# A second modulation panel multiplied in two halves around the first projection chunk

## The chip, the cores and the metric

The kernel runs on one core of one Trainium2 chip. The metric is the device time of one execution in microseconds (us). Before the change the median of three runs is 671.01 us (669.97 to 671.13).

## The reference, cut to what matters

One layer of a hybrid diffusion backbone works on 512 latent and 128 context tokens, each a row of 1024 numbers. Everything is float32. The part that the change touches is the beginning:

```
mod = SiLU(cond) @ w_mod + b_mod      # shift1, scale1, gate1, shift2, scale2, gate2; cond: c (latent), c_ctx (context)
h   = RMSNorm_pre1(x) * (1 + scale1) + shift1
z   = h @ w_in                        # columns [q | k | v | B | C | u], 512 each
```

Attention (four heads with differential softmax), a short gated convolution, the projection w_o, a second norm with shift2 and scale2 and a mixture of 16 experts follow. Lambda, a scalar of the attention, comes from two dot products of 64 numbers and an exponential.

## The kernel before, in words

The engines run lists of instructions written out by hand, one for each engine; each engine issues its list in order, and semaphores tie them together. There is no planner: the order of the calls in the code is the order of the work.

The first stage makes h, transposed and split into two float32r parts (high and low), and multiplies it by the first 512 columns of w_in. The 1024 numbers of a row are cut into eight **chunks** k of 128. Chunk k of h needs its columns of shift1 and scale1; these come in four **panels** n, panel n holding the columns of chunks 2n and 2n+1. The steps and their names are:

- `mod_early(n)` (TensorE, L1726): panel n of w_mod times the two conditioning vectors, eight steps over k, in four row groups of one PSUM bank. Its weights come in four quarters, each by two transfers of SyncE's queue (L467), into eight slots; between the panels SyncE fetches the quarters of w_in (L494).
- `mod_rows_out(n)` (VectorE, L1214): adds the bias and copies the result out of PSUM.
- `mod_cols(n)` (TensorE, L1734): transposes it, so that shift and scale lie along partitions.
- `mod_columns(n)` (VectorE, L1220 to L1226): sums the row groups and makes A1 and B1; its last instruction raises `a1_ready`.
- `h_transposes(k)` (TensorE, L1770) and `ctx_transposes(f)` (L1763): transposes of the normed x into PSUM, latent tokens a chunk at a time, context tokens four chunks at a time.
- `h_chunk(k)` (ScalarE, L802 and L806): scales and shifts the latent rows of chunk k, then rounds the chunk to the high part. It waits for `a1_ready` and for the transposes of its chunk. `h_ctx(k)` (VectorE, L1236) scales the context rows.
- `h_lo(k)` (VectorE, L1241): the low part of chunk k; raises `hT_ctx`.
- `split_hi` (ScalarE, L787) and `split_lo` (VectorE, L1207): high and low part of a quarter of w_in.
- `z_first(k)` (TensorE, L1779): chunk k for the first three blocks of 128 tokens, three matmuls of 512 columns each, accumulated over the chunks in three PSUM banks. It waits for `hT_ctx`.

TensorE's order is: panel 0, transposes of the context and of chunks 0 and 1, columns 0, the two dot products for lambda (L1796, L1797), panel 1, chunk 0, columns 1, transposes 2 and 3, chunk 1, panel 2, chunk 2, columns 2, transposes of the context and of 4 and 5, chunk 3, panel 3, chunk 4, columns 3, transposes 6 and 7, chunks 5, 6 and 7. Then `z_rows(3)` (L1846) and the rest of the projections follow. VectorE's order for n from 1 is: rows of panel n out, low part of chunk 2n-1, low part of the quarter, columns, context rows of 2n, low part of 2n, context rows of 2n+1.

Of the kernel before, what the change touches and what calls it, by code (L numbers as in the profile page):

```python
# [29 lines left out]
P = 128  # L30
D = 1024
KC = D // P
# [4 lines left out]
H, DV, DQ = 4, 128, 64  # L37
# [9 lines left out]
MOD_EARLY = 4  # L47
# [16 lines left out]
def build(nc, a):  # L64
# [16 lines left out]
    with ctx:  # L81
        def sb(name, shape, dt=F32):
            return ctx.enter_context(nc.sbuf_tensor(name, shape, dt))
# [20 lines left out]
        ones = sb("ones", [P, P])  # L104
# [7 lines left out]
        ps = ctx.enter_context(nc.psum_tensor("ps", [P, 8, N], F32))  # L112
# [14 lines left out]
        def col(i, n=1):  # L127
            return small[:, i:i + n]
# [7 lines left out]
        lamp = col(99)  # L136
        nlam = col(100)
        epsc = col(101)
        lamw = col(102, 4)
# [81 lines left out]
        def early_slot(j):  # L221
            return qkv[:, (j % 8) * D:(j % 8 + 1) * D]
# [952 lines left out]
        def _(dve):  # L1175
            n_chain = [0]

            def link(ins):
                n_chain[0] += 1
                ins.then_inc(S["dve_chain"], 1)  # L1180
                dve.wait_ge(S["dve_chain"], n_chain[0])
# [10 lines left out]
            link(nc.vector.tensor_copy(small[:, 16:39], ps[:, 6, 0:23]))  # L1192
            link(ts(subg, subg, 1.0 - LAM_INIT, None, ALU.mult))
            tt(lamp, lamq[:, 0:1], lamq[:, 1:2], ALU.mult).then_inc(S["lam_prod"], 1)

            dve.wait_ge(S["rms1"], 1)
            link(nc.vector.reciprocal(rstd, rt))
# [3 lines left out]
            def split_lo(item):  # L1201
                kind, c, r = item
                n = place[kind, c]
                m = 6 * P if kind == "conv" else QUARTER
                slot, rslot = (4 * n + r) % SPLIT, at_ring[item] % RAW
                dve.wait_ge(S["hi"], 4 * n + r + 1)
                tt(spl[:, slot, 1, 0:m], raw[:, rslot, 0:m], spl[:, slot, 0, 0:m].bitcast(F32), ALU.subtract).then_inc(S["lo"], 1)  # L1207

            def mod_rows_out(n):
                dve.wait_ge(S["mod_q"], 4 * (n + 1))  # L1210
                if n >= 2:
                    dve.wait_ge(S["col_mm"], n - 1)
                both = lambda ap, m: ap.rearrange("p (s n) -> p s n", s=2)[:, :, m:m + CHUNK]
                tt(both(rows_early[n % 2], 0), both(ps[:, 4 + n % 2, :], 0), both(bias_early, n * CHUNK), ALU.add).then_inc(S["mod_ev"], 1)  # L1214

            def mod_columns(n):
                dve.wait_ge(S["col_mm"], n + 1)
                ks = slice(2 * n, 2 * n + 2)
                parts = ps[:, 4 + n % 2, :].rearrange("p (j g m) -> p j m g", j=4, g=4)[:, :, 0:2, :]
                link(nc.vector.reduce_sum(cols_early.rearrange("p (j c) -> p j c", c=2), parts, axis=AX))  # L1220
                sh = cols_early[:, 0:4].rearrange("p (k c) -> p c k", c=2)
                sc = cols_early[:, 4:8].rearrange("p (k c) -> p c k", c=2)
                nc.vector.tensor_copy(B1[:, :, ks], sh)
                stt(A1[:, 0, ks], sc[:, 0, :], 1.0, gpre1[:, ks], ALU.add, ALU.mult)
                link(stt(A1[:, 1, ks], sc[:, 1, :], 1.0, gpre1[:, ks], ALU.add, ALU.mult))
                ts(col(183), epsc, 1.0, None, ALU.mult).then_inc(S["a1_ready"], 1)  # L1226

            def hf_rows(k):
                return work[:, TOK * (k % 2):TOK * (k % 2 + 1)]

            def h_ctx(k):
                dve.wait_ge(S["h_trc"], k // 4 + 1)
                if k >= 2:
                    dve.wait_ge(S["hT_ctx"], k - 1)
                o = (k % 4) * P
                ts(hf_rows(k)[:, L_LAT:TOK], ps[:, 2, o:o + P], A1[:, 1, k:k + 1], B1[:, 1, k:k + 1],  # L1236
                   ALU.mult, ALU.add).then_inc(S["hf_ctx"], 1)

            def h_lo(k):
                dve.wait_ge(S["hT_lat"], k + 1)  # L1240
                tt(hS[:, 1, k, :], hf_rows(k), hS[:, 0, k, :].bitcast(F32), ALU.subtract).then_inc(S["hT_ctx"], 1)  # L1241
            dve.wait_ge(S["bmod_in"], 16)
            mod_rows_out(0)
            split_lo(("in", 0, 0))
            mod_columns(0)
            h_ctx(0)
            h_ctx(1)
            h_lo(0)
            dve.wait_ge(S["lam_mm"], 1)
            nc.vector.tensor_copy(lamw[:, 0:1], ps[:, 6, 0:1]).then_inc(S["lam_cp"], 1)  # L1250
            nc.vector.tensor_copy(lamw[:, 1:2], ps[:, 3, 0:1]).then_inc(S["lam_cp"], 1)
            for n in range(1, MOD_EARLY):
                mod_rows_out(n)
                h_lo(2 * n - 1)
                split_lo(("in", 0, n))
                mod_columns(n)
                h_ctx(2 * n)
                h_lo(2 * n)
                h_ctx(2 * n + 1)
            h_lo(KC - 1)  # L1260
            split_lo(SPLITS[2][0])

            def rope_rows(g):
# [446 lines left out]
        def _(pe):  # L1710
            mm = nc.tensor.matmul
# [3 lines left out]
                    pe.wait_ge(S["lo"], 4 * n + k // 2 + 1)  # L1715
            PASSES = ((0, 0), (0, 1), (1, 0))

            def mod_early(n):
                if n >= 2:
                    pe.wait_ge(S["a1_ready"], n - 1)  # L1720
                for k in range(KC):
                    j = 4 * n + k // 2
                    if k % 2 == 0:
                        pe.wait_ge(early[j % 8], 32 * (j // 8 + 1))
                    g = 32 * (k % 4)
                    ins = mm(ps[g:g + 32, 4 + n % 2, :], condz[:, k, :], early_slot(j)[:, (k % 2) * N:(k % 2 + 1) * N],  # L1726
                             start=(k < 4), stop=(k >= 4))
                    if k % 2:
                        ins.then_inc(S["mod_q"], 1)

            def mod_cols(n):
                pe.wait_ge(S["mod_ev"], n + 1)
                for j in range(4):
                    ins = nc.tensor.transpose(ps[:, 4 + n % 2, j * P:(j + 1) * P], rows_early[n % 2][:, j * P:(j + 1) * P], ident[:, :])  # L1734
                ins.then_inc(S["col_mm"], 1)
# [20 lines left out]
            def ctx_transposes(f):  # L1756
                if f == 0:
                    pe.wait_ge(S["xn_ready"], TB)
                else:
                    pe.wait_ge(S["hf_ctx"], 4)  # L1760
                for j in range(4):
                    k = 4 * f + j
                    ins = nc.tensor.transpose(ps[:, 2, j * P:(j + 1) * P], x[:, CTX, k * P:(k + 1) * P], ident[:, :])  # L1763
                ins.then_inc(S["h_trc"], 1)

            def h_transposes(k):
                if k >= 2:
                    pe.wait_ge(S["hf_lat"], k - 1)
                for b in range(4):
                    ins = nc.tensor.transpose(ps[:, k % 2, b * P:(b + 1) * P], x[:, b, k * P:(k + 1) * P], ident[:, :])  # L1770
                ins.then_inc(S["h_tr"], 1)

            def z_first(k):
                n = place["in", 0]
                pe.wait_ge(S["hT_ctx"], k + 1)
                part_ready(n, k)
                for g, bank in enumerate((3, 6, 7)):
                    for s, m in PASSES:
                        ins = mm(ps[:, bank, :], hS[:, s, k, g * P:(g + 1) * P], weight(n, k, m),  # L1779
                                 start=(k == 0 and s + m == 0), stop=(k == KC - 1 and s == 1))  # L1780
                    if k == KC - 1:
                        ins.then_inc(S["z_mm"], 1)
# [4 lines left out]
            pe.wait_ge(S["stage_in"], 16 * 7)  # L1787
            nc.tensor.transpose(ps[:, 6, 0:23], vrow, ident[0:23, 0:23]).then_inc(S["rows_tr"], 1)
            pe.wait_ge(S["cols_ready"], 2)
            mod_early(0)  # L1790
            ctx_transposes(0)
            h_transposes(0)
            h_transposes(1)
            mod_cols(0)
            pe.wait_ge(S["lam_prod"], 1)
            mm(ps[:, 6, 0:1], ones[0:DQ, :], lamp[0:DQ, :], start=True, stop=True)  # L1796
            mm(ps[:, 3, 0:1], ones[DQ:P, :], lamp[DQ:P, :], start=True, stop=True).then_inc(S["lam_mm"], 1)  # L1797
            mod_early(1)
            pe.wait_ge(S["lam_cp"], 2)
            z_first(0)  # L1800
            mod_cols(1)
            h_transposes(2)
            h_transposes(3)
            z_first(1)
            mod_early(2)
            z_first(2)
            mod_cols(2)
            ctx_transposes(1)
            h_transposes(4)
            h_transposes(5)  # L1810
            z_first(3)
            mod_early(3)
            z_first(4)
            mod_cols(3)
            h_transposes(6)
            h_transposes(7)
            z_first(5)
            z_first(6)
            z_first(7)

# [452 lines left out]
```

## Time and profile before

| | |
|---|---|
| median of three runs | 671.01 us |
| profiled execution | 670.32 us |
| its span | 668.3 us |
| TensorE busy | 638.8 us (96% of the span) |
| VectorE busy | 511.7 us (77%) |
| ScalarE busy | 415.9 us (62%) |
| moved by DMA | 188.16 MB, mean 282 GB/s |

The span is the time from the first to the last instruction that the profile shows; the execution's own time lies some 2 us above it. PE is TensorE's matmuls, PEld its weight loads, DVE is VectorE, ACT is ScalarE, SP is SyncE's queue. A float32 matmul appears as several records, so the panel's eight steps are 16 records. A chain entry or a timeline line merges neighbouring instructions of a line of the code.

### The profile page before, as it was taken

The numbers are of one execution on the slowest core, as the hardware profiler recorded it, in microseconds if no ns is written. First come the engines' busy times: TensorE is split into PE (matmuls) and PEld (weight loads), VectorE is DVE, ScalarE is ACT, GpSimd is POOL, SyncE is SP. The second block draws the span as 40 slices with busy tenths as digits, with TensorE's granted clock in tenths as the row PEclk, the third lists the DMA queues.
The fourth block names the chain that finished last, engine by engine and source line by source line (L and its number), as shares of the span: only waits on it lengthen the run. The fifth ranks groups of instructions, "written<-read, shape, count | busy, mean of one in ns | idle before, by whom it ended". The sixth has DMA issues, their size and how long they took to land.

```text
span 668.3 us, 11051 instructions
## 1 busy us (share of the span) xinstructions
PE 638.8 (96%) x3570; PEld 524.4 (78%) x3570; DVE 511.7 (77%) x755; ACT 415.9 (62%) x640; POOL 106.1 (16%) x172
## 2 busy tenths in 40 slices
PE   3999999999999999999998999999999999999993
PEld 0577767889999998888786788888888888888871
DVE  2666576757676767775778989898989899999976
ACT  5552122344747486763447588888888888888863
POOL 2041000065000000000014500000000000370341
PEclk9999999999999999999999999999999999999997
DMA  9975768549211134495499799999999999999776
GB/s 332 386 248 186 262 242 254 156 147 339 60 38 57 63 97 156 138 332 191 147 323 346 237 415 419 420 420 420 420 420 419 418 410 415 416 404 375 302 273 157
DMA packets 77147, 188.16 MB, mean 282 GB/s; under 512 B 7823, under 2 KB 29380, under 8 KB 77108
## 3 DMA queue, kind: packets, MB, share of 16 engines
q1 hardware_dynamic: 65408, 153.11, 61.7%
q0 software_dynamic: 7392, 22.47, 9.9%
q10 hardware_dynamic: 4310, 12.10, 4.5%
q8 instruction: 22, 0.36, 0.2%
q14 instruction: 15, 0.12, 0.1%
HBM read 166.12 MB, written 21.53 MB: 281 GB/s over the span
## 4 chain that ended last, share of the span: by engine, by line
PE 81%; DVE 6%; DMA 5%; ACT 2%; SPq 2%; issue 2%; POOL 1%; ACTq 0%; DVEq 0%; POOLq 0%
PE ps L2135 23%; PE ps L2155 12%; PE ps L1846 10%; PE ps L1870 7%; PE ps L1902 6%; PE ps L1874 5%; PE ps L1923 3%; PE ps L1946 2%; PE ps L1779 2%; PE ps L2111 2%; SPq L467 2%; PE ps L1937 2%; DMA catT_mem<-token_rows,token_lists 1%; PE ps L1744 1%; DMA catT_mem<-expert_rows,early_slots 1%
## 5 line engine op out<-in xcount | busy, mean ns | idle before, releaser
L2135 PE MATMUL ps<-split_ring,split_rows 128*128 128x512 f32 x714 | 167.0, 392 | 0.1
L1492 DVE TENSOR_TENSOR split_ring<-qkv_mem,split_ring 128x1024 fp32r<-128x1024 f32 x123 | 142.9, 1221 | 23.2 <-ACT split_ring L975 23.2
L2135 PEld LDWEIGHTS ps<-split_ring,split_rows 128*128 128x128 f32 x714 | 132.7, 188 | 28.2 <-DVE split_ring L1492 0.5
L975 ACT CAST split_ring<-qkv_mem 128x1024 fp32r<-128x1024 f32 x123 | 120.1, 1053 | 9.3 <-ACT catT_mem L1081 9.3
L1870 PE MATMUL ps<-split_rows,split_ring 128*128 128x384 f32 x288 | 87.1, 349 | 0.2 <-ACT work L910 0.2
L2155 PE MATMUL ps<-split_ring,split_rows 128*128 128x512 f32 x360 | 86.4, 395 | 0.0
L2155 PEld LDWEIGHTS ps<-split_ring,split_rows 128*128 128x128 f32 x360 | 66.6, 188 | 13.7
L1874 PE MATMUL ps<-split_rows,split_ring 128*128 128x256 f32 x288 | 77.0, 280 | 0.0
L1492 DVE TENSOR_TENSOR split_ring<-raw_ring,split_ring 128x1024 fp32r<-128x1024 f32 x64 | 74.2, 1218 | 0.0
L1846 PE MATMUL ps<-split_ring,split_rows 128*128 128x512 f32 x288 | 68.0, 393 | 0.0
L975 ACT CAST split_ring<-raw_ring 128x1024 fp32r<-128x1024 f32 x64 | 62.4, 1047 | 1.2 <-DMA raw_ring<-in_w_exp_up 1.2
L1846 PEld LDWEIGHTS ps<-split_ring,split_rows 128*128 128x128 f32 x288 | 53.4, 188 | 10.8
L787 ACT CAST split_ring<-raw_ring 128x1024 fp32r<-128x1024 f32 (+1 forms) x36 | 34.2, 958 | 40.7 <-DMA raw_ring<-in_w_in 40.7
L1902 PE MATMUL ps<-split_ring,split_rows 128*128 128x512 f32 x240 | 58.4, 396 | 0.7 <-DVE split_ring L1207 0.7
L1207 DVE TENSOR_TENSOR split_ring<-raw_ring,split_ring 128x1024 fp32r<-128x1024 f32 (+1 forms) x36 | 39.4, 1102 | 23.1 <-ACT split_ring L787 22.9
L1870 PEld LDWEIGHTS ps<-split_rows,split_ring 128*128 128x128 f32 x288 | 53.5, 189 | 1.4 <-issue 1.2
L1874 PEld LDWEIGHTS ps<-split_rows,split_ring 128*128 128x128 f32 x288 | 53.4, 188 | 0.0
L1902 PEld LDWEIGHTS ps<-split_ring,split_rows 128*128 128x128 f32 x240 | 44.0, 188 | 10.4 <-DVE split_ring L1207 1.0
L1348 DVE TENSOR_REDUCE small<-ps 128x1 f32<-128x640 f32 (+1 forms) x40 | 26.8, 712 | 12.9 <-PE ps L1923 12.7
L631 POOL DMA_DIRECT2D x_rows<-in_b_mod x10 | 5.1, 512 | 181.7 <-DMA out_lat<-x_rows 181.7
L679 POOL TENSOR_TENSOR rows_now<-token_lists 128x1 uint32<-128x1 uint32 x13 | 4.8, 368 | 182.2 <-PE ps L2111 182.2
L878 ACT COPY x_rows<-ps 128x640 f32<-128x640 f32 (+1 forms) x20 | 12.2, 612 | 32.0 <-PE ps L1937 31.9
(363 smaller groups left out, 924.3 us busy)
## 6 DMA issues: line engine op xcount, KB each, us to landing
qkv_mem<-in_w_exp_gate SPq DMA_DIRECT2D x64, 512.0 KB, 8.4
qkv_mem<-in_w_exp_up SPq DMA_DIRECT2D x60, 512.0 KB, 7.0
raw_ring<-in_w_exp_down SPq DMA_DIRECT2D x60, 512.0 KB, 8.3
raw_ring<-in_w_mod SPq DMA_DIRECT2D x26, 512.0 KB, 4.2
qkv_mem<-in_w_mod SPq DMA_DIRECT2D x32, 256.0 KB, 7.0
expert_rows<-catT_mem ACTq DMA_DIRECT2D x14, 512.0 KB, 6.6
expert_rows<-work POOLq DMA_DIRECT2D x26, 256.0 KB, 5.8
raw_ring<-in_w_in SPq DMA_DIRECT2D x12, 512.0 KB, 6.9
```

The source lines that it names most:

```text
L787: nc.scalar.copy(spl[:, (4 * n + r) % SPLIT, 0, 0:m], raw[:, q % RAW, 0:m]).then_inc(S["hi"], 1)
L975: nc.scalar.copy(moe_split(tile, j, r, 0), moe_raw(tile, j, r)).then_inc(S["hi"], 1)
L1207: tt(spl[:, slot, 1, 0:m], raw[:, rslot, 0:m], spl[:, slot, 0, 0:m].bitcast(F32), ALU.subtract).then_inc(S["lo"], 1)
L1348: nc.vector.reduce_max(nm[:, u % 2, c:c + 1], psf[:, SC[c]:SC[c] + nk], axis=AX, negate=True).then_inc(S["neg_max"], 1)
L1492: tt(moe_split(tile, j, r, 1), moe_raw(tile, j, r), moe_split(tile, j, r, 0).bitcast(F32), ALU.subtract).then_inc(S["lo"], 1)
L1846: ins = mm(ps[:, g % 2, :], hS[:, s, k, b * P:(b + 1) * P], weight(n, k, m), start=(k == 0 and s + m == 0), stop=(k == KC - 1 and s == 1))
L1870: return mm(ps[:, CONV_BANK, 0:LOW], conv_weight(n, k, s, part), hS[:, m, k, 0:LOW], start=(k == 0 and s + m == 0), stop=(k == KC - 1 and ...
L1874: return mm(ps[:, CONV_BANK + 1, 0:HIGH], conv_weight(n, k, s, part), hS[:, m, k, LOW:TOK], start=(k == 0 and s + m == 0), stop=(k == KC - ...
L1902: ins = mm(ps[:, banks + j, :], cS[:, s, b, kk, :], weight(place["o", j], kk, m), start=(kk == 0 and s + m == 0), stop=(kk == KC - 1 and s ...
L1923: ins = mm(psf[:, SC[c] + o:SC[c] + o + m], q[rows, :], key[rows, :], start=(s + w == 0), stop=(s == 1))
L2135: ins = mm(ps[:, j, :], rows[:, s, k * P:(k + 1) * P], moe_split(tile, j, k // 2, m)[:, (k % 2) * N:(k % 2 + 1) * N], start=(k == 0 and s ...
L2155: ins = mm(ps[:, 5 + half, :], aS[:, s, k, :], spl[:, moe_split_slot(turn, j, k), m, half * N:(half + 1) * N], start=(k == 0 and s + m == ...
```

## The change

Four things are reordered; no arithmetic is added or taken away.

1. The two dot products for lambda and VectorE's two copies of them go ahead of panel 0.
2. Columns 0 go ahead of the transposes of chunk 1. Panel 1 is cut into steps 0 to 3, which stay ahead of chunk 0, and steps 4 to 7, which go behind it.
3. Columns 1, 2 and 3 go into the middle of a chunk (1, 3 and 4), between its first block of tokens and the other two. Panel 2 goes behind chunk 2, panel 3 ahead of chunk 4 and behind chunk 3, the transposes of chunks 6 and 7 behind chunk 5.
4. VectorE's order becomes, for every n: rows out, columns, context rows of 2n, low part of the quarter, low part of 2n, context rows of 2n+1, low part of 2n+1.

```diff
 # VectorE
+            dve.wait_ge(S["lam_mm"], 1)
+            nc.vector.tensor_copy(lamw[:, 0:1], ps[:, 6, 0:1]).then_inc(S["lam_cp"], 1)
+            nc.vector.tensor_copy(lamw[:, 1:2], ps[:, 3, 0:1]).then_inc(S["lam_cp"], 1)
             dve.wait_ge(S["rms1"], 1)
...
-            mod_rows_out(0)
-            split_lo(("in", 0, 0))
-            mod_columns(0)
-            h_ctx(0)
-            h_ctx(1)
-            h_lo(0)
...
-            for n in range(1, MOD_EARLY):
+            for n in range(MOD_EARLY):
                 mod_rows_out(n)
-                h_lo(2 * n - 1)
-                split_lo(("in", 0, n))
                 mod_columns(n)
                 h_ctx(2 * n)
+                split_lo(("in", 0, n))
                 h_lo(2 * n)
                 h_ctx(2 * n + 1)
-            h_lo(KC - 1)
+                h_lo(2 * n + 1)
 # TensorE
-            def mod_early(n):
+            def mod_early(n, ks=range(KC)):
-            def z_first(k):
+            def z_first(k, gs=range(3)):
...
             pe.wait_ge(S["cols_ready"], 2)
+            pe.wait_ge(S["lam_prod"], 1)
+            mm(ps[:, 6, 0:1], ones[0:DQ, :], lamp[0:DQ, :], start=True, stop=True)
+            mm(ps[:, 3, 0:1], ones[DQ:P, :], lamp[DQ:P, :], start=True, stop=True).then_inc(S["lam_mm"], 1)
             mod_early(0)
             ctx_transposes(0)
             h_transposes(0)
+            mod_cols(0)
             h_transposes(1)
-            mod_cols(0)
...
-            mod_early(1)
+            mod_early(1, range(4))
             pe.wait_ge(S["lam_cp"], 2)
             z_first(0)
+            mod_early(1, range(4, KC))
+            h_transposes(2)
+            z_first(1, (0,))
             mod_cols(1)
-            h_transposes(2)
+            z_first(1, (1, 2))
             h_transposes(3)
-            z_first(1)
+            z_first(2)
             mod_early(2)
-            z_first(2)
+            z_first(3, (0,))
             mod_cols(2)
+            z_first(3, (1, 2))
             ctx_transposes(1)
             h_transposes(4)
             h_transposes(5)
-            z_first(3)
             mod_early(3)
-            z_first(4)
+            z_first(4, (0,))
             mod_cols(3)
+            z_first(4, (1, 2))
+            z_first(5)
             h_transposes(6)
             h_transposes(7)
-            z_first(5)
             z_first(6)
             z_first(7)
```

## Rows read from the trace of the kernel before

**Rows 1.** The page: busy times of the engines, and the chain by engine.
```profile
PE 638.8 (96%) x3570; PEld 524.4 (78%) x3570; DVE 511.7 (77%) x755; ACT 415.9 (62%) x640; POOL 106.1 (16%) x172
...
PE 81%; DVE 6%; DMA 5%; ACT 2%; SPq 2%; issue 2%; POOL 1%; ACTq 0%; DVEq 0%; POOLq 0%
```
**Rows 2.** Waits of PE after 49 us: total, times, longest.
```profile
PE ps L2111 <- DMA catT_mem<-token_rows,token_lists: 2.4, 1, 2.4
```
**Rows 3.** Windows: length, busy us of each engine, granted clock, DMA share, GB/s.
```profile
12.00:24.00 12.00, 11.05 (x53) 3.55 (x54) 7.74 (x19) 5.41 (x8) 0.00 (x0) 1.00 1.08 389
24.00:38.00 14.00, 14.00 (x88) 10.07 (x91) 9.30 (x22) 7.29 (x10) 0.00 (x0) 1.00 1.08 392
...
80.00:120.00 40.00, 40.00 (x199) 29.62 (x199) 28.56 (x41) 10.49 (x16) 1.98 (x4) 1.00 0.77 250
```
**Rows 4.** Timeline of PE, first stage: start, us, instructions, idle before and releaser.
```profile
12.16 4.96 PE L1726 MATMUL ps<-qkv_mem,cond_columns 128*32 128x512 f32 x16 [2.59 <-DMA qkv_mem<-in_w_mod]
...
17.71 1.04 PE L1770 MATMUL ps<-ident,x_rows 128*128 128x128 f32 x8
18.58 0.60 PE L1734 MATMUL ps<-ident,catT_mem 128*128 128x128 f32 x4
19.11 0.27 PE L1796 MATMUL ps<-small,ones 64*128 64x1 f32 x1
...
19.43 1.70 PE L1726 MATMUL ps<-qkv_mem,cond_columns 128*32 128x512 f32 x8
...
20.07 0.14 PEld L1726 LDWEIGHTS ps<-qkv_mem,cond_columns 128*32 128x32 f32 x4 [0.50 <-DMA qkv_mem<-in_w_mod]
...
22.82 1.05 PE L1726 MATMUL ps<-qkv_mem,cond_columns 128*32 128x512 f32 x4 [0.30 <-DMA qkv_mem<-in_w_mod]
...
45.32 4.45 PE L1779 MATMUL ps<-split_ring,split_rows 128*128 128x512 f32 x18 [0.28 <-DVE split_rows L1241]
```
**Rows 5.** Chain of waits, 31 to 50 us: start, us, what.
```profile
31.39 2.27 PE ps L1779 x9
...
34.54 0.87 PE ps L1770 x8
...
37.48 1.85 PE ps L1726 x16
...
41.64 0.45 PE ps L1734 x4
...
42.87 0.79 ACT work L802
...
44.43 0.84 DVE split_rows L1241
```
**Rows 6.** Timeline of ACT and DVE around chunk 4.
```profile
35.06 0.78 ACT L802 ACTIVATE work<-ps,small 128x512 f32<-128x512 f32 x1 [3.16 <-PE ps L1770]
36.63 0.82 DVE L1241 TENSOR_TENSOR split_rows<-work,split_rows 128x640 fp32r<-128x640 f32 x1 [1.43 <-ACT split_rows L806]
37.37 0.40 DVE L1236 TENSOR_SCALAR work<-ps,small 128x128 f32<-128x128 f32 x1
37.87 0.72 ACT L806 CAST split_rows<-work 128x640 fp32r<-128x640 f32 x1 [0.59 <-DVE work L1236]
39.43 0.69 DVE L1214 TENSOR_TENSOR catT_mem<-ps,catT_mem 128x512 f32<-128x512 f32 x1 [1.65 <-PE ps L1726]
```
**Rows 7.** Timeline of DVE, 13 to 20 us.
```profile
13.53 0.19 DVE L1197 RECIPROCAL small<-small 128x5 f32<-128x5 f32 x1 [3.36 <-ACT small L792]
17.23 0.69 DVE L1214 TENSOR_TENSOR catT_mem<-ps,catT_mem 128x512 f32<-128x512 f32 x1
18.42 1.23 DVE L1207 TENSOR_TENSOR split_ring<-raw_ring,split_ring 128x1024 fp32r<-128x1024 f32 x1 [0.49 <-ACT split_ring L787]
```
**Rows 8.** Timeline of SyncE's queue: issues of the fourth panel.
```profile
24.38 5.84 SPq L467 DMA_DIRECT2D qkv_mem<-in_w_mod  x8
```
**Rows 9.** Transfers: issues, KB each, median us to landing.
```profile
qkv_mem<-in_w_mod SPq DMA_DIRECT2D x32, 256.0 KB, 7.0
```

More of the change, by code:

```diff
@@ L1242, in _ @@
             dve.wait_ge(S["bmod_in"], 16)
-            mod_rows_out(0)
-            split_lo(("in", 0, 0))
-            mod_columns(0)
-            h_ctx(0)
-            h_ctx(1)
-            h_lo(0)
-            dve.wait_ge(S["lam_mm"], 1)
-            nc.vector.tensor_copy(lamw[:, 0:1], ps[:, 6, 0:1]).then_inc(S["lam_cp"], 1)
-            nc.vector.tensor_copy(lamw[:, 1:2], ps[:, 3, 0:1]).then_inc(S["lam_cp"], 1)
-            for n in range(1, MOD_EARLY):
+            for n in range(MOD_EARLY):
                 mod_rows_out(n)
-                h_lo(2 * n - 1)
-                split_lo(("in", 0, n))
                 mod_columns(n)
                 h_ctx(2 * n)
+                split_lo(("in", 0, n))
                 h_lo(2 * n)
                 h_ctx(2 * n + 1)
-            h_lo(KC - 1)
+                h_lo(2 * n + 1)
             split_lo(SPLITS[2][0])
@@ L1716, in _ @@
             PASSES = ((0, 0), (0, 1), (1, 0))
-            def mod_early(n):
+            def mod_early(n, ks=range(KC)):
                 if n >= 2:
                     pe.wait_ge(S["a1_ready"], n - 1)
-                for k in range(KC):
+                for k in ks:
                     j = 4 * n + k // 2
@@ L1776, in z_first @@
                 part_ready(n, k)
-                for g, bank in enumerate((3, 6, 7)):
+                for g in gs:
+                    bank = (3, 6, 7)[g]
                     for s, m in PASSES:
@@ L1792, in _ @@
             h_transposes(0)
+            mod_cols(0)
             h_transposes(1)
-            mod_cols(0)
-            pe.wait_ge(S["lam_prod"], 1)
-            mm(ps[:, 6, 0:1], ones[0:DQ, :], lamp[0:DQ, :], start=True, stop=True)
-            mm(ps[:, 3, 0:1], ones[DQ:P, :], lamp[DQ:P, :], start=True, stop=True).then_inc(S["lam_mm"], 1)
-            mod_early(1)
+            mod_early(1, range(4))
             pe.wait_ge(S["lam_cp"], 2)
             z_first(0)
+            mod_early(1, range(4, KC))
+            h_transposes(2)
+            z_first(1, (0,))
             mod_cols(1)
-            h_transposes(2)
+            z_first(1, (1, 2))
             h_transposes(3)
-            z_first(1)
+            z_first(2)
             mod_early(2)
-            z_first(2)
+            z_first(3, (0,))
             mod_cols(2)
+            z_first(3, (1, 2))
             ctx_transposes(1)
```

## The prediction

> **What bounds the kernel now.** I read the page first: TensorE (PE) is busy for 96% of the span, and PE makes up 81% of the chain that ended last [rows 1]. So time is lost or won where PE stands still. The list of PE's waits after 49 us comes second: the longest is 2.4 us [rows 2]. Windows of the projections behind the first stage show PE busy throughout, 40.00 of 40 us from 80 to 120 [rows 3], so a shift of the first stage should run through to the end. Third, the timeline of PE in the first stage. Panel 0 of the modulation weights ends at 17.12 us. Panel 1 then runs in pieces: eight records from 19.43, its second quarter's weight load at 20.07 and its last four records at 22.82, with "DMA qkv_mem" named as what ended the gaps [rows 4]. Here PE waits for weights. The DMA share of this stretch is 1.08, and the stream stays full until 38 us [rows 3]. The reader is to see a wait of about 3 us ahead of the first projection chunk (23.87 us, that is 22.82 and 1.05 more), that PE is then busy for all of the window from 24 to 38 [rows 3], and a gap of 0.28 us before chunk 6 at 45.32 [rows 4]. Fourth, the chain of waits around that small gap. It goes from the last columns (mod_cols 3, ends 42.09) through DVE's reduction and A1 to ACT's scaled copy (42.87), and through ACT's rounding cast and DVE's low part (44.43) to chunk 6 [rows 5]. That is **3.23 us from the end of the columns to the first matmul that can use them**. The same path from the end of the transposes of a chunk, when its columns are long there, can be read at chunk 4: the pair of transposes begins at 34.54 and takes 0.87, so chunk 4's end at 34.97; ACT starts at 35.06, the low part ends at 37.45 [rows 6]. With 0.05 us to PE (the low part before chunk 6 ends at 45.27, chunk 6 starts at 45.32 [rows 4, 5]) that is **2.53 us from the end of the transposes**. Both latencies are now covered by work that PE has in between. The question for every moved line is whether that cover stays.
>
> **The change, part by part.** All times are those of the profiled execution (span 668.30, its own time 670.32). The work of PE is the same; what is moved decides.
>
> *Lambda.* The records of L1796 and L1797 leave PE's path between 19.11 and 19.43 [rows 4], which is 0.3 us. They go to before 12.16, where PE stood idle 2.59 us; the two small DVE copies go into DVE's idle 3.36 us before 13.53 [rows 7]. Cost nothing, and if that cover were gone 0.3 us.
>
> *Columns of panel 0 ahead of the second transposes.* A group of four transposes costs 0.44 (mod_cols 3: 41.64 to 42.09 [rows 5]). After the context transposes and one group from 17.71, mod_cols(0) runs at 18.14 instead of 18.58 [rows 4]; its operand is ready at 17.92, as the evacuation begins at 17.23 and takes 0.69 [rows 7]. It ends at 18.58, and 3.23 later, 21.81, the first chunk may start. On DVE the quarter's low part (1.23 us [rows 7]) now stands behind the context rows and fits exactly into the time in which ACT works.
>
> *Panel 1 in halves.* The first half needs the second quarter, which landed at 20.07 [rows 4], and is done by 21. The first chunk goes at 21.81 instead of 23.87: **2.06 us won**. A chunk takes 2.27 (from 31.39 [rows 5]), so it ends at 24.08. The second half follows. The trace has no half of a panel with its data there. Bounds: 0.92 (not less, as the matmuls are the same), half of the 1.85 of panel 3 (37.48 to 39.34 [rows 5]), and 1.05, a single quarter alone [rows 4]. I take 0.92, since all four row groups are filled as in a whole panel. It ends at 25.0 against 23.87: the panel is 1.1 late, but one chunk ahead.
>
> *Columns inside chunks, to chunk 2.* Transposes to 25.4, a third of chunk 1 to 26.1, mod_cols(1) to 26.55 (before: 26.57). Chunk 2 can start 3.23 later, at 29.78. Ahead of it PE has two thirds of chunk 1 (1.33: six of nine matmuls in the 2.07 that a chunk takes behind transposes: 35.41, where the pair from 34.54 ends, to 37.48 [rows 5]) and one group of transposes: done at 28.3. **PE waits 1.5.** Before, panel 2 filled this time; now it stands behind chunk 2. Chunk 2 ends at 32.05, panel 2 at 33.9. Before, the same work was done at 33.66 (31.39 and 2.27 [rows 5]): the lead is gone, +0.2.
>
> *Chunk 3 and panel 3.* A third of chunk 3 (0.76) to 34.66. The evacuation of panel 2 takes 0.09 to start, 0.69 and 0.05 to PE, so mod_cols(2) runs from 34.73 to 35.17. The rest of chunk 3 to 36.5, context transposes, transposes of chunk 4 to **37.37** and of 5 to 37.8, panel 3 to 39.65 (before 39.34). Its weights are no limit: the fourth panel was issued by 30.2 and a quarter takes 7.0 us to land [rows 8, 9], so the last is there near 37.2, before 37.8. Chunk 4 may start 2.53 after its transposes, at 39.9: a wait of 0.25. Its first third ends at 40.66.
>
> *mod_cols(3) and DVE's order.* mod_cols(3) needs DVE's evacuation of panel 3. In the new order of DVE that stands **behind the low part of chunk 5**, which was behind it before (evacuation at 39.43 [rows 6]). From 37.37 the path is: low part of 4 (ends +2.48), context rows of 5 (begin +2.40), cast of 5 (+2.90 to +3.62), low part of 5 (from +3.65), evacuation (from +4.38, ends +5.07), PE at +5.11. These offsets are those of rows 6 against 34.97, with the low part and the evacuation changing places. So mod_cols(3) starts at 42.48, and **PE waits 1.8**; behind it in PE's order are all the chunks that could run. It ends at 42.92. Two thirds of chunk 4 to 44.25, chunk 5 to 46.52.
>
> *Transposes of chunks 6 and 7 behind chunk 5.* They stood ahead of it, and chunk 5 covered the 2.53 us. Now chunk 6's end at 46.96, chunk 7's at 47.4, and chunk 6 can start at 49.49: **PE waits 2.1**. For chunk 7 ACT and DVE have the 2.2 us of chunk 6; before it ran on without a gap, 18 matmuls in 4.45 [rows 4], so the stage ends at 53.94 against 49.77.
>
> The sum is +4.2 us. Queues: SP's quarters of panel 3 wait for panel 1's matmuls, at the latest for 25.0, and the later half of panel 3 was issued after 27 [rows 8]; POOL's loads behind the last A1 start 0.9 later, and what uses them, behind chunk 7, moves by 4.2. The bounds on the parts: each of the three paths (3.23, 5.11, 2.53) could be 0.1 shorter (two of its wakes of 0.05 gone) or 0.4 longer (half of the low part of a quarter, 1.23 [rows 7], in DVE's way); with the half panel, 0.13, that is +3.9 to +5.5.
>
> *The clock.* In 12 to 24 us the granted clock is 1.00, the 2.4 GHz level, though PE waited for DMA several times [rows 3]. The Trainium skill ("TensorE: Matmul & The Clock Gate", section "HAM oscillation — how this bites in real kernels") warns that matmul bursts with waits between them can fall back to the half clock; this trace does not show it here, and it is a rival below.
>
> **The rivals.** *B, not slower:* the waits before chunk 2, mod_cols(3) and chunk 6 don't appear, because what bounds those chunks is only the columns, which now come earlier relative to the matmuls that use them. For it: the chain of before leads from A1 to ACT for chunk 6 (ACT starts at 42.87, 0.78 behind the columns' end [rows 5]). Against it: ACT also needs the transposes, and those of 6 are issued behind chunk 5. The new waits sum to 5.7, so without them 4.2 - 5.7 = -1.5, or 669.5 on the median. It decides when these waits stay under 1.5 in all.
>
> *C, given back later:* a later wait of PE that doesn't move with PE swallows a part. The longest is the 2.4 us for gathered token rows [rows 2]; this leaves +1.8, 672.8. Against it: that gather starts from rows that PE's own results produce, so it moves along.
>
> *D, the clock falls in the waits:* after the waits of 1.8 and 2.1 us the last 18 matmuls run at 1.2 GHz. The trace has no such row; at half the clock their 4.45 is doubled (an estimate from that row), +8.6, 679.7.
>
> *E, the stream sets the stage:* if the weights' landing, not PE, fixed the stage's end, nothing changes, 671.0. Against it: after 23.87 PE has no gap until 38 us [rows 3], and the one before 45.32 ended on DVE [rows 4].
>
> **How the numbers follow.** The profiled execution took 670.32, 0.7 below the median of 671.01. On the median, 671.01 + 4.2 = 675.2. Chances: forecast 0.75 (own range 674.6 to 676.5), B 0.09, C 0.08, D 0.03, E 0.05. The range from 672.6 to 676.7 takes in the forecast and C and leaves out B, D and E. About 0.2%, 1.3 us, can be told from no change: faster 0.09 (B), the same 0.05 (E), slower 0.86 (forecast, C, D).
>
> **What would show it.** In the changed profile the first L1779 starts near 21.8 (right: the halves work). A gap of PE of 1.5 before the third chunk; a gap of 1.8 before the last L1734, with DVE's L1214 running right behind an L1241 and not ahead of it; a gap of 2.1 before the last 18 L1779, ended by L1241; the first L1846 near 54 instead of 49.6, and the same spacing from there to the end. I am wrong if the last 18 L1779 follow the transposes without a gap, if L1846 starts before 50, or if the later list of waits has shrunk by what the first stage lost.

## The result, and the profile after

The changed kernel takes 676.48 us in the median of seven runs (673.24 to 678.48), the kernel before in the same comparison 669.97 (668.79 to 671.13). The ratio is 1.0091, with an interval from 1.0074 to 1.0108: it is **slower by 6.1 us**, between 5.0 and 7.2. Forecast were 4.2 us and 675.2; the direction and the three waits were right, the size was too small.

The page of the changed kernel, busy times and chain by engine, and below it PE's longest wait behind the first stage, answer to [rows 1, 2]:

```profile
PE 640.6 (95%) x3570; PEld 525.7 (78%) x3570; DVE 512.1 (76%) x755; ACT 416.2 (62%) x640; POOL 106.3 (16%) x172
...
PE 83%; DVE 7%; ACT 4%; issue 3%; DMA 1%; ACTq 1%; DVEq 0%; POOLq 0%
```
```profile
PE ps L2109 <- DMA catT_mem<-token_rows,token_lists: 2.4, 1, 2.4
```

PE has the same number of instructions, 1.8 us more of busy time, and a smaller share of a longer span. The wait for token rows is 2.4 us as before: nothing was given back there. The timeline of PE in the first stage (start, us, instructions, idle before and its releaser) answers to [rows 4]; L1719 is mod_early, L1727 mod_cols, L1763 the transposes, L1773 z_first, L1844 the first z_rows:

```profile
22.13 2.31 PE L1773 MATMUL ps<-split_ring,split_rows 128*128 128x512 f32 x9 [1.24 <-DVE split_rows L1244]
24.37 1.06 PE L1719 MATMUL ps<-qkv_mem,cond_columns 128*32 128x512 f32 x8
...
30.39 2.35 PE L1773 MATMUL ps<-split_ring,split_rows 128*128 128x512 f32 x9 [1.41 <-DVE split_rows L1244]
...
40.90 0.98 PE L1773 MATMUL ps<-split_ring,split_rows 128*128 128x512 f32 x3 [0.25 <-DVE split_rows L1244]
43.50 0.76 PE L1727 MATMUL ps<-ident,catT_mem 128*128 128x128 f32 x4 [1.62 <-DVE catT_mem L1217]
43.91 5.29 PE L1773 MATMUL ps<-split_ring,split_rows 128*128 128x512 f32 x15
49.04 1.04 PE L1763 MATMUL ps<-ident,x_rows 128*128 128x128 f32 x8
52.17 4.43 PE L1773 MATMUL ps<-split_ring,split_rows 128*128 128x512 f32 x18 [2.10 <-DVE split_rows L1244]
56.44 5.60 PE L1844 MATMUL ps<-split_ring,split_rows 128*128 128x512 f32 x24
```

The reader is to see four long gaps and a short one of 0.25 before chunk 4, which all end on DVE: 1.24 us before chunk 0, 1.41 before chunk 2, 1.62 before mod_cols(3) and 2.10 before chunk 6. Before, PE's time was lost ahead of chunk 0, in pieces that ended on DMA: panel 1 took 4.4 us from 19.43 instead of the 1.9 of a panel whose weights are there [rows 4]. The first z_rows matmul starts at 56.44; before it was 49.60, so the stage ends 6.8 us later. One line fits none of the forecast's terms: fifteen matmuls of chunks 4 and 5 take 5.29 us, though nine take 2.3 elsewhere. The windows of one microsecond (length, busy us of each engine, granted clock, DMA share, GB/s) say why:

```profile
43.00:44.00 1.00, 0.50 (x5) 0.51 (x5) 0.44 (x1) 0.00 (x0) 0.00 (x0) 0.95 0.01 4
44.00:45.00 1.00, 1.00 (x5) 0.81 (x4) 0.63 (x5) 0.00 (x0) 0.00 (x0) 0.50 0.00 0
45.00:46.00 1.00, 1.00 (x4) 0.81 (x3) 0.66 (x3) 0.00 (x0) 0.67 (x1) 0.50 0.00 0
46.00:47.00 1.00, 1.00 (x3) 0.76 (x3) 0.90 (x1) 0.00 (x0) 1.00 (x2) 0.50 0.02 8
47.00:48.00 1.00, 1.00 (x5) 0.82 (x4) 0.00 (x0) 0.00 (x0) 1.00 (x3) 0.84 0.69 184
```

Behind the wait before mod_cols(3) the granted clock is 0.50, the 1.2 GHz level, until some way into 47 to 48 us. DVE's timeline shows what that wait is for: the evacuation of panel 3 (L1217) runs right behind the low part of chunk 5 (L1244), although panel 3 had been done at 40.65; in [rows 6] it ran first.

```profile
42.02 0.83 DVE L1244 TENSOR_TENSOR split_rows<-work,split_rows 128x640 fp32r<-128x640 f32 x1 [0.85 <-ACT split_rows L806]
42.76 0.68 DVE L1217 TENSOR_TENSOR catT_mem<-ps,catT_mem 128x512 f32<-128x512 f32 x1
```

### The profile page after: what moved, and what is told of

The parts are those of the page before. It is cut to its first block, busy times and chain, and to the rows that moved or that the text cites. A ratio compares the mean times of both kernels' runs of the same rounds, so it can differ in the third digit from the quotient of the medians.

```text
span 674.2 us, 11052 instructions
## 1 busy us (share of the span) xinstructions
PE 640.6 (95%) x3570; PEld 525.7 (78%) x3570; DVE 512.1 (76%) x755; ACT 416.2 (62%) x640; POOL 106.3 (16%) x172
## 4 chain that ended last, share of the span: by engine, by line
PE 83%; DVE 7%; ACT 4%; issue 3%; DMA 1%; ACTq 1%; DVEq 0%; POOLq 0%
PE ps L2133 24%; PE ps L2153 12%; PE ps L1844 10%; PE ps L1868 7%; PE ps L1900 6%; PE ps L1872 5%; PE ps L1921 3%; PE ps L1944 2%; PE ps L2109 2%; PE ps L1935 2%; PE ps L1773 2%; DMA catT_mem<-token_rows,token_lists 1%; PE ps L1737 1%; PE ps L2141 1%; PE ps L1824 1%
## 5 line engine op out<-in xcount | busy, mean ns | idle before, releaser
L1844 PE MATMUL ps<-split_ring,split_rows 128*128 128x512 f32 x288 | 68.0, 393 | 0.0
L1844 PEld LDWEIGHTS ps<-split_ring,split_rows 128*128 128x128 f32 x288 | 53.4, 188 | 10.9
```

The lines of the kernel that those rows point to most:

```text
L1844: ins = mm(ps[:, g % 2, :], hS[:, s, k, b * P:(b + 1) * P], weight(n, k, m), start=(k == 0 and s + m == 0), stop=(k == KC - 1 and s == 1))
```

## The experiments

Times against the kernel before are worked out from the ratio and its interval (0.001 is 0.67 us).

**Transposes of chunks 6 and 7 back ahead of chunk 5.**

```diff
+            h_transposes(6)
+            h_transposes(7)
             z_first(5)
-            h_transposes(6)
-            h_transposes(7)
             z_first(6)
```

> The changed kernel with one part undone: the transposes of chunks 6 and 7 stand ahead of chunk 5 again. Theory A (the loss is three waits of PE for work that the new order no longer covers, 1.4 us before chunk 2, 1.6 before mod_cols(3), 2.1 before chunk 6, and a fall of the clock behind the second of them, worth 1.7): the wait of 2.1 us before chunk 6 goes, the other two and the low clock behind mod_cols(3) stay; the first z_rows matmul near 54.5 us instead of 56.4, the time about 4.4 us above the kernel before. Theory B (the cuts cost by themselves: chunk 4 and 5's fifteen matmuls took 5.3 us since they stand in pieces): the same 2.1 us. Theory C (the last columns, not the transposes, hold chunk 6): the wait stays, at most 0.5 us won.

Ratio 1.0072 (1.0044 to 1.0101), 4.8 us above the kernel before. Timeline of PE:

```profile
43.62 0.66 PE L1727 MATMUL ps<-ident,catT_mem 128*128 128x128 f32 x4 [1.63 <-DVE catT_mem L1217]
44.04 2.71 PE L1773 MATMUL ps<-split_ring,split_rows 128*128 128x512 f32 x6
...
47.90 6.64 PE L1773 MATMUL ps<-split_ring,split_rows 128*128 128x512 f32 x27
54.38 5.60 PE L1844 MATMUL ps<-split_ring,split_rows 128*128 128x512 f32 x24
```

Chunks 5, 6 and 7 now run as one line of 27 without a gap: the 2.1 us are gone, 56.44 became 54.38. Theory C falls; the other wait is untouched, with a low clock behind it again: the six matmuls behind it take 2.71 us, and six at full clock take 1.64.

**Evacuation of panel 3 back ahead of the low part of chunk 5.**

```diff
                 mod_rows_out(n)
+                if n == 3:
+                    h_lo(5)
                 mod_columns(n)
...
-                h_lo(2 * n + 1)
+                if n != 2:
+                    h_lo(2 * n + 1)
```

> The changed kernel with one part undone: on VectorE the evacuation of panel 3 stands ahead of the low part of chunk 5 again. Theory A: PE waits under 0.2 us before mod_cols(3), the granted clock stays at 1.00 and the fifteen matmuls of chunks 4 and 5 take about 3.7 us; first z_rows matmul near 53.1, time about 3.2 us above the kernel before. Theory B: the 1.6 us of the wait go, but the fifteen matmuls still take 5.3 us: 54.8, about 4.9 above the kernel before.

Ratio 1.0086 (1.0055 to 1.0117), 5.8 us above: less was won than either theory said. By the interval (3.7 to 7.8) theory B's 4.9 would fit; the timeline of PE and a window of two microseconds decide against it:

```profile
41.85 0.66 PE L1730 MATMUL ps<-ident,catT_mem 128*128 128x128 f32 x4
42.26 3.68 PE L1776 MATMUL ps<-split_ring,split_rows 128*128 128x512 f32 x15
...
48.91 6.00 PE L1776 MATMUL ps<-split_ring,split_rows 128*128 128x512 f32 x18 [2.09 <-DVE split_rows L1244]
54.74 5.61 PE L1847 MATMUL ps<-split_ring,split_rows 128*128 128x512 f32 x24
```
```profile
50.00:52.00 2.00, 2.00 (x7) 1.59 (x6) 1.85 (x2) 1.89 (x2) 2.00 (x5) 0.55 0.20 49
```

The wait before mod_cols(3) is gone, and the fifteen matmuls take 3.68 us in the same pieces: theory B's 5.3 falls. But the low clock came behind the next wait, before chunk 6, and its 18 matmuls took 6.00 us instead of 4.43. So the low clock is not tied to one of the waits. Theory A's 53.1 and 3.2 us were missed all the same, since it counted on a clock of 1.00.

**Both together.** The edit is the sum of the two above.

> Both parts undone together. Theory A: waits before mod_cols(3) and chunk 6 gone, clock at 1.00, first z_rows matmul near 51.0, about 1.5 us above the kernel before; what is left is the wait of 1.4 us before chunk 2. Theory B: 52.7, about 3.1 above.

Ratio 1.0020 (1.0003 to 1.0036), 1.3 us above the kernel before, as theory A said; theory B's 3.1 lies outside the interval of 0.2 to 2.4 us. The profiled execution was the slowest of its twelve (674.03). Its timeline has the low clock in a third place, behind 1.85 us of waiting before chunk 0, whose nine matmuls took 3.59 us:

```profile
22.14 3.59 PE L1776 MATMUL ps<-split_ring,split_rows 128*128 128x512 f32 x9 [1.85 <-DVE split_rows L1244]
...
31.95 2.37 PE L1776 MATMUL ps<-split_ring,split_rows 128*128 128x512 f32 x9 [1.41 <-DVE split_rows L1244]
...
46.07 6.75 PE L1776 MATMUL ps<-split_ring,split_rows 128*128 128x512 f32 x27
52.65 5.60 PE L1847 MATMUL ps<-split_ring,split_rows 128*128 128x512 f32 x24
```

The two waits are gone, as theory A has it. The stage's end, 52.65, is the number of theory B, but not by its mechanism: from the start of chunk 0 to the end of the half panel behind it this execution takes 1.6 us more than the changed kernel's (4.79 against 3.23), and without that it is 51.1, theory A's 51.0.

**Panel 2 ahead of chunk 2 as well: three parts undone.**

```diff
+            mod_early(2)
             z_first(2)
-            mod_early(2)
             z_first(3, (0,))
```

> The changed kernel with three parts undone: transposes of chunks 6 and 7 ahead of chunk 5, evacuation of panel 3 ahead of the low part of chunk 5, and panel 2 ahead of chunk 2 again. The halves of panel 1 and the columns inside chunks stay. Theory A (uncovered waits): the wait of 1.4 us before chunk 2 goes as well; without a fall of the clock the first z_rows matmul is near 49.9 (49.6 in the kernel before), the time within 0.5 us of the kernel before. Theory B (the cuts cost by themselves): 1.5 us or more above it.

Ratio 1.0002 (0.9988 to 1.0016): no difference from the kernel before. Timeline of PE:

```profile
28.95 1.92 PE L1722 MATMUL ps<-qkv_mem,cond_columns 128*32 128x512 f32 x16
30.80 3.03 PE L1776 MATMUL ps<-split_ring,split_rows 128*128 128x512 f32 x12
...
49.25 5.60 PE L1847 MATMUL ps<-split_ring,split_rows 128*128 128x512 f32 x24
```

Panel 2 fills the time that the wait before chunk 2 had, and the stage ends at 49.25 (49.60 before). The halves of panel 1 and the columns inside chunks are still in this kernel. So the cuts, taken together with the earlier first chunk, cost nothing that can be measured, and the three moves that were undone make up the whole loss. One move that the list of the change doesn't name, though its diff has it, is also still in: the transposes of chunks 4 and 5 stand behind chunk 3. It leaves a wait of 0.24 us before chunk 4.

**One part alone, put into the kernel before: transposes of 6 and 7 behind chunk 5.**

> The kernel before with one part of the change alone: the transposes of chunks 6 and 7 behind chunk 5. Theory A: PE waits 2.1 us before chunk 6 instead of 0.28, first z_rows matmul near 51.4 instead of 49.6, the time 1.8 us above the kernel before, clock at 1.00 (in the changed kernel the wait of 2.1 us before chunk 6 was not followed by a low clock). Rival (any wait of about 2 us lowers the clock): a low clock behind it and up to 1.7 us more, 3.5 above.

Ratio 1.0053 (1.0035 to 1.0072), 3.5 us above the kernel before, more than the 1.8 of the wait. Timeline of PE:

```profile
47.46 4.43 PE L1779 MATMUL ps<-split_ring,split_rows 128*128 128x512 f32 x18 [2.10 <-DVE split_rows L1241]
51.73 5.61 PE L1846 MATMUL ps<-split_ring,split_rows 128*128 128x512 f32 x24
```

The wait is 2.10 instead of 0.28 and the stage ends 2.1 us later. This execution had no low clock in the first stage. It had one much later, behind PE's wait for token rows:

```profile
365.00:370.00 5.00, 2.54 (x11) 2.32 (x11) 2.05 (x2) 1.83 (x4) 4.14 (x10) 0.78 0.97 370
370.00:375.00 5.00, 5.00 (x23) 4.11 (x22) 3.95 (x5) 3.44 (x5) 4.46 (x7) 0.88 0.28 107
```

This profile's span is 3.1 us longer than that of the kernel before. From the end of the wait for token rows to the 24 matmuls of the mixture that follow PE takes 9.94 us, 9.38 before, so 0.6 us come from there. The last output transfer takes 8.1 us from its issue to the end of the span, 6.0 before; in between 1.7 us are won back. Eight of the thirteen profiles have the late low stretch, with and without the move of this experiment; the first ones of the kernel before and of the changed kernel have not.

**The same with the wait filled.** Eight matmuls into an unread PSUM bank stand in it.

```diff
             h_transposes(7)
+            for d in range(8):
+                mm(ps[:, 4, :], hS[:, 0, 0, 0:P], weight(0, 0, 0), start=True, stop=True)
             z_first(6)
```

> The kernel before with the transposes of chunks 6 and 7 behind chunk 5 (as e4_late_transposes_alone) and eight matmuls more in the wait that this makes; they write a PSUM bank that nobody reads, so only PE's idle time is taken away. Theory A with the clock (PE's standing still is what lets the clock fall in some executions, and that is why e4 lost 3.5 us where the wait is 1.8): the wait is as long as before in time, but the median is 1.9 us above the kernel before. Rival (e4's further loss is not the clock's): 3.5 us above, as e4.

Ratio 1.0039 (1.0022 to 1.0055), 2.6 us above. Timeline of PE:

```profile
45.27 2.08 PE L1819 MATMUL ps<-split_ring,split_rows 128*128 128x512 f32 x8
47.61 4.43 PE L1779 MATMUL ps<-split_ring,split_rows 128*128 128x512 f32 x18 [0.27 <-DVE split_rows L1241]
51.88 5.61 PE L1848 MATMUL ps<-split_ring,split_rows 128*128 128x512 f32 x24
```

It lies between the two expectations, and the unfilled kernel was measured once more:

> The kernel before with the transposes of chunks 6 and 7 behind chunk 5, again: 2.1 us of PE's wait before chunk 6, and 2 to 3.5 us above the kernel before; a low clock behind the wait in the profile, or none, by chance.

Ratio 1.0033 (1.0014 to 1.0051), 2.2 us above. The two measurements of the unfilled kernel differ by more than the filled one differs from either: **this pair decides nothing**, and what the 3.5 us had beyond the 2.1 of the stage isn't shown to come from the order.

**The changed kernel, twice more.**

> The changed kernel as it is, on the same chip and in the same call. Theory A with the clock: the same three waits of 1.4, 1.6 and 2.1 us, since they are set by the order; a stretch of half clock of some 3.4 us, at another of the waits than the one behind mod_cols(3) or at none; 5 to 6.5 us above the kernel before. Rival (the low clock belongs to the cut matmuls of chunks 4 and 5): again at 44 to 47 us.

Ratio 1.0113 (1.0083 to 1.0142), 7.6 us above (5.5 to 9.5), more than the 5 to 6.5 expected. The profiled execution is the fastest of its six (674.09). Timeline of PE:

```profile
22.34 2.32 PE L1773 MATMUL ps<-split_ring,split_rows 128*128 128x512 f32 x9 [0.79 <-DVE split_rows L1244]
...
43.73 0.66 PE L1727 MATMUL ps<-ident,catT_mem 128*128 128x128 f32 x4 [1.62 <-DVE catT_mem L1217]
44.14 3.68 PE L1773 MATMUL ps<-split_ring,split_rows 128*128 128x512 f32 x15
...
50.79 4.41 PE L1773 MATMUL ps<-split_ring,split_rows 128*128 128x512 f32 x18 [2.10 <-DVE split_rows L1244]
55.04 5.60 PE L1844 MATMUL ps<-split_ring,split_rows 128*128 128x512 f32 x24
```

The same kernel, the same waits to a hundredth before chunk 2, mod_cols(3) and chunk 6, and no low clock in this stage: the fifteen matmuls take 3.68 us and the stage ends at 55.04. Only the wait before chunk 0 differs, 0.79 us instead of 1.24. **In the first stage the order alone is worth 55.04 - 49.60 = 5.4 us**; a low stretch in this stage adds 5.29 - 3.68 = 1.6 when it comes, and the first profile without it gives 5.2. These are differences of single timelines against the one of the kernel before.

**The changed kernel with its four waits filled, beside a third measurement of it unfilled.**

```diff
             pe.wait_ge(S["lam_cp"], 2)
+            mm(ps[:, 7, :], ident[:, :], x[:, 0, 0:N], start=True, stop=True)
             z_first(0)
...
             h_transposes(3)
+            fill(5)
             z_first(2)
...
             z_first(4, (0,))
+            fill(6)
             mod_cols(3)
...
             h_transposes(7)
+            fill(8)
             z_first(6)
```

> The changed kernel with matmuls more in its four waits (one float32 matmul before chunk 0, five, six and eight of 512 columns before chunk 2, mod_cols(3) and chunk 6); they write PSUM banks that nobody reads at that time. Theory A with the clock (the order costs 5.4 us of the first stage, as in after_again without a low clock there; what the time has beyond it, about 1 us in the middle of the runs, is half clock that only some executions have behind PE's waits): no low clock in the first stage, first z_rows matmul near 55.2, median 5.4 to 5.8 above the kernel before, and 0.5 to 1.5 below after_third. Rival (the further microsecond is not the clock's): the same time as after_third, 6.5 above.

> The changed kernel as it is, beside after_filled on the same chip: 6 to 7 us above the kernel before, with or without a low clock in the profiled execution's first stage (near 56.4 or 55.0 for the first z_rows matmul).

Filled: ratio 1.0057 (1.0035 to 1.0078), 3.8 us above (2.3 to 5.2), median 673.56; unfilled: 1.0077 (1.0055 to 1.0100), 5.2 above (3.7 to 6.7), median 675.15. Both lie below what was expected (5.4 to 5.8, and 6 to 7). Timeline of PE, filled:

```profile
43.55 0.66 PE L1727 MATMUL ps<-ident,catT_mem 128*128 128x128 f32 x4 [0.26 <-DVE catT_mem L1217]
43.96 3.71 PE L1773 MATMUL ps<-split_ring,split_rows 128*128 128x512 f32 x15
...
54.92 5.61 PE L1852 MATMUL ps<-split_ring,split_rows 128*128 128x512 f32 x24
```

The stage ends where it ends unfilled without a low clock (55.04), with 1.6 us less in the median. The mean granted clock of the execution is 0.994 or more in five of the seven filled runs and in one of the six unfilled (this mean also counts the end of the execution, where PE has finished). The medians fit the clock's part, but the two intervals overlap from 1.0055 to 1.0078, so the amount is not settled. It also stays open why a stage that ends 5.3 us later comes with a time only 3.8 above: the interval ends at 5.2. The unfilled profile of this comparison had the low stretch behind mod_cols(3) again.

**What the change wins, alone, in the old order.** Lambda and columns 0 stay where the change put them, panel 1 stays in halves; the rest of PE's order is that of the kernel before, but for columns 3. On DVE the low part of chunk 2n-1 stands behind the evacuation of panel n again.

```diff
                 mod_rows_out(n)
+                if n >= 1:
+                    h_lo(2 * n - 1)
                 mod_columns(n)
...
             h_transposes(2)
-            z_first(1, (0,))
+            h_transposes(3)
             mod_cols(1)
-            z_first(1, (1, 2))
-            h_transposes(3)
+            z_first(1)
+            mod_early(2)
             z_first(2)
-            mod_early(2)
-            z_first(3, (0,))
             mod_cols(2)
-            z_first(3, (1, 2))
             ctx_transposes(1)
             h_transposes(4)
             h_transposes(5)
+            z_first(3)
             mod_early(3)
-            z_first(4, (0,))
+            z_first(4, (0, 1))
             mod_cols(3)
-            z_first(4, (1, 2))
-            z_first(5)
+            z_first(4, (2,))
             h_transposes(6)
             h_transposes(7)
+            z_first(5)
             z_first(6)
```

> The order of the kernel before, with what the change wins alone: lambda first, columns 0 ahead of the transposes of chunk 1, panel 1 in halves around chunk 0; transposes 2 and 3 cover the evacuation of panel 1; columns 3 between the second and third block of chunk 4. Theory A: the first chunk starts at 22.1 as in the changed kernel, no wait of PE over 0.4 us behind it, first z_rows matmul near 47.7, the time 1.9 us below the kernel before (ratio 0.997). Rival (the stream of weights sets the pace once PE leads: panels 2 and 3 land too late): gaps in L1719 that end on DMA, and 0 to 1 us won.

Ratio 0.9993 (0.9977 to 1.0010): not to be told from the kernel before. Theory A failed; the time fits the rival's 0 to 1 us, but not its cause. Timeline of PE, and below it two lines of DVE:

```profile
22.18 2.29 PE L1775 MATMUL ps<-split_ring,split_rows 128*128 128x512 f32 x9 [1.68 <-DVE split_rows L1244]
24.39 1.07 PE L1721 MATMUL ps<-qkv_mem,cond_columns 128*32 128x512 f32 x8
25.39 1.09 PE L1765 MATMUL ps<-ident,x_rows 128*128 128x128 f32 x8
...
27.03 2.33 PE L1775 MATMUL ps<-split_ring,split_rows 128*128 128x512 f32 x9
...
49.19 5.60 PE L1844 MATMUL ps<-split_ring,split_rows 128*128 128x512 f32 x24
```
```profile
25.55 0.69 DVE L1217 TENSOR_TENSOR catT_mem<-ps,catT_mem 128x512 f32<-128x512 f32 x1 [3.15 <-PE ps L1721]
26.16 0.81 DVE L1244 TENSOR_TENSOR split_rows<-work,split_rows 128x640 fp32r<-128x640 f32 x1
```

No gap ended on DMA behind chunk 0, so the stream was not the cause. I had reckoned the early start of chunk 0 (22.18 against 23.80) as won, but the second half of the panel still has to run: 1.0 us, from 24.39 to 25.39. That leaves 0.6 of the 1.6 us. At chunk 1 the lead is down to 0.2 us (27.03 against 27.20), as chunk 1 also waits for its low part (DVE, 26.16), which in this order stands behind the evacuation of panel 1 although DVE had been idle for 3.15 us ahead of it. With the gap before chunk 6 gone the stage ends 0.4 us earlier. PE's wait for weights had only become a wait of 1.68 us for chunk 0's rows. No version was found that is measurably faster than the kernel before; this one with the low part of chunk 1 ahead of that evacuation was not run.

## Why the prediction was right, and where its sizes were off

- *First chunk:* 21.81 forecast, 22.13 measured. The step held. DVE's reduction starts at 18.88; the forecast has it right behind the columns at 18.6. The "wait of about 3 us" ahead of this chunk is 2.6 by its own rows (panel 1 takes 4.44 us instead of 1.85); the sum does not use it.
- *Wait before chunk 2:* 1.5 forecast, 1.41 measured. The start, 30.39 instead of 29.78, was 0.6 late: 0.3 from the first chunk, and the rest from the half panel (24.37 to 25.36, 0.99 for 0.92) and the transposes behind it (0.59 for 0.44).
- *mod_cols(2):* 34.73 forecast, 35.44 measured.
- *Wait of chunk 4:* 0.25 forecast and measured. *Wait before mod_cols(3):* 1.8 forecast, 1.62 measured, and ended by L1217 behind L1244 as forecast. It starts at 43.50 instead of 42.48.
- *Wait before chunk 6:* 2.1 forecast, 2.10 measured. With the experiments the steps are shown, not only argued: undoing the two last moves takes the loss from 6.1 to 1.3 us, undoing the third as well to 0.1. The third was not undone alone, and the intervals of 1.3 (0.2 to 2.4) and 0.1 (-0.8 to 1.1) overlap; for its 1.4 us stands the timeline, where the wait is gone.
- *The stage's end:* a shift of 4.2 was forecast. Without a low clock it is 5.2 to 5.4. The term that was too small is the work between the waits, not the waits: those came out as forecast or shorter. In the first profile chunk 0 is 0.3 late, chunk 2 another 0.3, mod_cols(2) 0.1 and chunk 4 0.3; from there on nothing is added. In the chain of waits (start, us, what) two groups of four transposes show part of it, those of chunk 2 and mod_cols(2): they take 0.59 and 0.62, where the sum has 0.44. Why is not shown.

```profile
25.43 0.59 PE ps L1763 x4
...
35.49 0.62 PE ps L1727 x4
```

- *Passing through:* right up to the last stage. PE's longest wait later stayed at 2.4 us, and the mixture of experts started 6.9 us later, its first 24 matmuls at 381.54 instead of 374.65 in the two profiled executions. These differ at the end by 5.8 us, and the traces show where the rest went. In the execution before, DVE waits 2.13 us near the end for rows of the experts, and PE behind it for DVE:

```profile
651.65 1.98 PE L2180 MATMUL ps<-x_rows,ident 128*128 128x512 f32 x4 [0.92 <-DVE x_rows L1665]
```

  The changed kernel's profile has neither wait, and its last output is issued only 5.0 us later (667.34 against 662.30); from there to the end of the span it takes 6.9 us instead of 6.0. Neither is shown to follow from the order: the kernel with three parts undone reaches this stage 0.2 us later than the kernel before and has no such wait either, and the last output takes between 5.5 and 8.9 us in the thirteen profiles.
- *The clock:* rival D, at 0.03, came true in part. The step that failed is reading one clean execution ("1.00 in 12 to 24 us") as if waits of PE left the clock alone, so that the sum has no term for it. The price given, the last 18 matmuls doubled, was also too high: the low stretch costs 1.6 us, and only in some executions. The Trainium skill ("TensorE: Matmul & The Clock Gate", section "HAM oscillation — how this bites in real kernels") warns of matmul bursts with waits between them; its own case has waits for DMA of about 3 to 5 us, and here they were 1.6 to 2.1. In the first stage the profiles of the changed kernel agree in two of three executions, and in one they don't.

That the time, 676.48, lies in the stated range of 672.6 to 676.7 is luck in part. The loss of 6.1 us is above the forecast's own upper bound of 5.5, and added to the 671.01 that the forecast started from it would be 677.1; in the comparison the kernel before took 669.97. (The lower end of the own range, 674.6, does not come out of the sum either: 671.01 and 3.9 are 674.9.)

The 5.4 us of order lie inside the measured interval (5.0 to 7.2) by themselves, and inside that of the third measurement (3.7 to 6.7), but just below that of the second (5.5 to 9.5) and above that of the filled kernel (2.3 to 5.2). How much of the 0.7 us up to the middle of the first is the clock's is not settled.

## What to carry to other kernels

Before moving an instruction on an engine that issues in order, take two latencies from the trace, from the event that releases it to the first consumer that can run, and count what stands between them in the new order; a producer moved behind the work that used to cover it shows up as a wait of just the uncovered part. Look at the queue of the other engine as well: the second wait came from an evacuation that stood behind a low part on DVE, not from anything on PE. And work that must run anyway and only starts earlier in two pieces is a lead of the first piece minus the second, here 0.6 us out of 1.6, of which 0.2 was left at the next chunk.

## What the runs showed of the hardware

The changed kernel, with the same three waits behind chunk 0, ran with and without a stretch at the 1.2 GHz level in the first stage. Over the kernels that differ from it by one or two moves the stretch came behind different waits: behind 1.62 us before mod_cols(3) (clock 0.50 from 44 to 47 us), behind 2.09 us before chunk 6 (0.55 from 50 to 52) and behind 1.85 us before chunk 0. Each cost 1.6 us. Eight of the thirteen profiles have another behind the wait of 2.0 to 2.5 us for token rows (0.78 and 0.88 in the windows shown), which cost 0.3 to 0.7 us.

The profile of the kernel before shows no such stretch ahead of 660 us, where PE has finished. Its mean clock in single runs lies between 0.989 and 0.996, and its runs between 667.4 and 673.5 us; that these are low stretches is not shown, for the mean clock also counts the end without matmuls (0.50 to 0.59 from 660 us on), and that end is as long as the last output takes, 5.5 to 8.9 us. A difference of a microsecond is thus only to be read from many runs, or from the timeline of a stretch whose clock is known.
